# A mixer, attention and mixture-of-experts layer on one core: the gate as one activation, and the whole down product ahead of the remaining transposes

## What is computed

```python
p = softmax(q @ k.T * HD ** -0.5)            # 4 heads, 256 memory tokens
o = p @ v
# for each block of up to 128 slots of one expert
gu = xb @ w_gu + b_gu
g, u = gu[:, :D_FF], gu[:, D_FF:]
g = jnp.minimum(g, SWIGLU_LIMIT)
u = jnp.clip(u, -SWIGLU_LIMIT, SWIGLU_LIMIT)
h = (u + 1.0) * (g * jax.nn.sigmoid(SWIGLU_ALPHA * g))     # SWIGLU_ALPHA = 1.702
return h @ w_down + b_down
```

## Time and profile before

| | |
|---|---|
| median of 3 runs | 2306.88 us (2304.44 to 2308.20) |
| profiled execution | 2305.12 us |
| its span, first to last instruction | 2303.4 us |
| mean granted TensorE clock | 0.975 |
| TensorE, VectorE, ScalarE busy | 2187.8, 1662.6, 1261.9 us |
| instructions | 33358 |

### The profile page before, as it was taken

How to read it: one execution, slowest core, us unless ns; L and a number is a source line. 1 busy time by engine, 2 the same in 40 slices (tenths; PEclk the granted TensorE clock), 3 DMA queues, 4 the chain that set the end, 5 groups by cost and what they waited for, 6 DMA issues and landing times.

```text
span 2303.4 us, 33358 instructions
## 1 busy us (share of the span) xinstructions
PE 2187.8 (95%) x9450; PEld 1665.3 (72%) x9451; DVE 1662.6 (72%) x1641; ACT 1261.9 (55%) x1192; POOL 425.3 (18%) x357
## 2 busy tenths in 40 slices
PE   7999999998998699999999999999999999999986
PEld 4555678886454588877787878788778787887873
DVE  5655842406134899887789977998889779997883
ACT  3146251413213477666567756776677567775663
POOL 0791000000000112122112112221222112221110
PEclk9999999998998799999999999999999999999997
DMA  5103331111123499989799979999899799997984
GB/s 170 37 1 112 110 146 37 37 37 37 57 101 139 170 385 381 324 312 324 244 318 380 369 277 331 350 369 335 311 315 374 275 305 373 380 379 276 311 304 161
DMA packets 233715, 555.95 MB, mean 241 GB/s; under 512 B 19972, under 2 KB 20200, under 8 KB 232200
## 3 DMA queue, kind: packets, MB, share of 16 engines
q1 hardware_dynamic: 218448, 512.41, 61.0%
q0 software_dynamic: 13264, 42.63, 7.4%
q10 hardware_dynamic: 1960, 0.35, 0.1%
HBM read 518.38 MB, written 33.69 MB: 240 GB/s over the span
## 4 chain that ended last, share of the span: by engine, by line
PE 83%; DVE 8%; issue 6%; ACT 2%; DVEq 1%; ACTq 1%; DMA 0%
PE PS L959 21%; PE PS L627 19%; PE PS L963 11%; PE PS L980 11%; PE PS L987 6%; PE PS L785 4%; PE PS L825 4%; DVE WL L1887 2%; PE PS L1012 2%; PE PS L951 2%; PE PS L917 1%; PE PS L645 1%; PE PS L1040 1%; DVE WA L1428 1%; DVE XEL L1883 0%
## 5 line engine op out<-in xcount | busy, mean ns | idle before, releaser
L1887 DVE TENSOR_TENSOR WL<-WA,WH 128x2048 fp32r<-128x2048 f32 x288 | 654.7, 2286 | 66.1 <-ACT WH L1327 62.8
L1887 DVE TENSOR_TENSOR WL<-H,WH 128x2048 fp32r<-128x2048 f32 x144 | 329.3, 2288 | 55.3 <-ACT WH L1306 48.0
L959 PE MATMUL PS<-WH,XEH 128*128 128x512 f32 x1344 | 361.7, 391 | 0.0
L1327 ACT CAST WH<-WA 128x2048 fp32r<-128x2048 f32 x140 | 267.2, 1909 | 164.2 <-PE PS L987 162.2
L963 PE MATMUL PS<-WL,XEH 128*128 128x512 f32 x1344 | 351.9, 389 | 0.0
L959 PE MATMUL PS<-WH,XEL 128*128 128x512 f32 x1152 | 309.4, 390 | 0.0
L959 PEld LDWEIGHTS PS<-WH,XEH 128*128 128x128 f32 x1344 | 253.5, 189 | 51.6
L963 PEld LDWEIGHTS PS<-WL,XEH 128*128 128x128 f32 x1344 | 252.7, 188 | 52.7
L959 PEld LDWEIGHTS PS<-WH,XEL 128*128 128x128 f32 x1152 | 217.2, 189 | 46.1
L980 PE MATMUL PS<-WH,HTH 128*128 128x512 f32 x672 | 191.0, 407 | 6.3 <-DVE WL L1887 6.3
L1311 ACT CAST WH<-WA 128x2048 fp32r<-128x2048 f32 x72 | 137.2, 1910 | 76.2 <-PE PS L963 75.8
(11 more groups left out here) (323 smaller groups left out, 2931.5 us busy)
## 6 DMA issues: line engine op xcount, KB each, us to landing
WA<-in_exp_w_gu SPq DMA_DIRECT2D x216, 1024.0 KB, 7.4
H<-in_exp_w_gu SPq DMA_DIRECT2D x72, 1024.0 KB
WA<-in_exp_w_down SPq DMA_DIRECT2D x72, 1024.0 KB, 7.3
H<-in_exp_w_down SPq DMA_DIRECT2D x72, 1024.0 KB, 8.3
WB<-in_xa_wkv SPq DMA_DIRECT2D x4, 2048.0 KB, 7.9
WB<-in_w_in SPq DMA_DIRECT2D x3, 2048.0 KB, 9.3
y_acc<-H SPq DMA_DIRECT2D x9, 512.0 KB, 2.6
H<-in_x SPq DMA_DIRECT2D x4, 1024.0 KB, 6.0
```

Source lines behind the costliest of these rows:

```text
L959: nc.tensor.matmul(PS[:, 2 * h + t, :], x[:, KT4 * half + k, t * P:(t + 1) * P], WH[:, j % 4, k * HALF:(k + 1) * HALF], start=False, stop= ...
L1327: nc.scalar.copy(WH[:, s, :], raw_gu(s)).then_inc(gu_high, 1)
L1887: v.tensor_tensor(WL[:, s, :], src, WH[:, s, :].bitcast(F32), sub).then_inc(done, 1)
```

## The change

It has five parts.

1. The gate: sigmoid on ScalarE into `SIG` and product on VectorE become one activation in place, `Gelu_apprx_sigmoid` (x times sigmoid of 1.702 x), with one semaphore (`gate_done`) for two; its table is loaded ahead of the loop in place of the sigmoid's. `gate_times` goes. The upper rows of the up product now have a buffer of their own, `UPH`.
2. TensorE's round: both pairs of down slices directly behind one another; token transposes of half 1 and both groups of hidden transposes behind them.
3. VectorE's round: low tokens of half 0 ahead of `down_low(3)`; `down_low(2)` keeps its place ahead of `hidden` of half 1.
4. Attention: the copies of the transposed weights (`keep`) move from VectorE to ScalarE, behind the exponentials.
5. `GF3` is made on ScalarE ahead of the loop and not on VectorE after it.

```diff
@@ -394,8 +394,8 @@
-        g_min, sig_done, gs_done, u_clip, h_done = (
-            sem("g_min"), sem("sig_done"), sem("gs_done"), sem("u_clip"), sem("h_done"))
+        g_min, gate_done, u_clip, h_done = (
+            sem("g_min"), sem("gate_done"), sem("u_clip"), sem("h_done"))
@@ -1017,9 +1017,9 @@
                 by_tiles(pe, n_n, next_tokens(0))
                 by_tiles(pe, n_p, down(0))
+                by_tiles(pe, n_p, down(2))
                 by_tiles(pe, n_n, next_tokens(1))
                 by_tiles(pe, n_i, hidden_transposes(0))
-                by_tiles(pe, n_p, down(2))
                 by_tiles(pe, n_i, hidden_transposes(1))
@@ -1239,6 +1239,13 @@
+            def keep(n):
+                l, hp = att[n]
+                u = ("pt", l, hp)
+                wait_filled(act, u)
+                evac(act, nc.scalar.copy(PT[:, 2 * hp:2 * hp + 2, :, l * P:(l + 1) * P],
+                                         bank(u).rearrange("p (h m t) -> p h m t", h=2, m=MT)), u)
@@ -1253,6 +1260,10 @@
+                if n >= LEAD:
+                    keep(n - LEAD)
+            for n in range(len(att) - LEAD, len(att)):
+                keep(n)
@@ -1275,7 +1286,7 @@
-                    nc.scalar.preload_act_table(ACT.Sigmoid)
+                    nc.scalar.preload_act_table(ACT.Gelu_apprx_sigmoid)
@@ -1293,6 +1304,9 @@
+            act.wait_ge(gf_done, 1)
+            nc.scalar.copy(GF3.rearrange("p l (r e) -> p l r e", r=3), GF.unsqueeze(2).to_broadcast([P, L, 3, E])) \
+                .then_inc(gf3_done, 1)
@@ -1333,17 +1347,15 @@
                     act.wait_ge(g_min, 4 * i + 2 * half + 2)
-                    act.wait_ge(gs_done, 2 * i + half + 1)
                     for t in range(tiles):
                         n = HP if t else P
-                        ins = nc.scalar.activation(SIG[0:n, t, :], HS[0:n, t, half * HALF:(half + 1) * HALF], ACT.Sigmoid,
-                                                   scale=ALPHA)
-                    ins.then_inc(sig_done, 1)
+                        g_t = HS[0:n, t, half * HALF:(half + 1) * HALF]
+                        ins = nc.scalar.activation(g_t, g_t, ACT.Gelu_apprx_sigmoid)
+                    ins.then_inc(gate_done, 1)
                 def upper_up(half):
                     act.wait_ge(gu_used, 8 * i + 4 * half + 8)
-                    act.wait_ge(gs_done, 2 * i + half + 2)
-                    nc.scalar.copy(SIG[0:HP, 1, :], PS[HP:P, 3, :]).then_inc(halves_moved, 1)
+                    nc.scalar.copy(UPH[0:HP, :], PS[HP:P, 3, :]).then_inc(halves_moved, 1)
@@ -1725,20 +1737,11 @@
-            for n in range(len(att) + LEAD):
+            for n in range(len(att) + 1):
                 if n < len(att):
                     maxima(n)
-                if 0 < n <= len(att):
+                if n > 0:
                     normalise(n - 1)
-                if n >= LEAD:
-                    keep(n - LEAD)
@@ -1933,26 +1935,18 @@
-                def gate_times(half, tiles):
-                    dve.wait_ge(sig_done, 2 * i + half + 1)
-                    for t in range(tiles):
-                        n = HP if t else P
-                        g_t = HS[0:n, t, half * HALF:(half + 1) * HALF]
-                        ins = v.tensor_tensor(g_t, g_t, SIG[0:n, t, :], mul)
-                    ins.then_inc(gs_done, 1)
-                    dve.wait_ge(gs_done, 2 * i + half + 2)
+                    dve.wait_ge(gate_done, 2 * i + half + 1)
@@ -1963,7 +1957,6 @@
                     gate_up_low(5)
-                    gate_times(0, tiles)
                     gate_up_low(6)
@@ -1992,14 +1985,12 @@
                     down_low(1)
-                by_tiles(dve, n_i, lambda tiles: gate_times(1, tiles))
-                with dve.If_cmp(n_p, 0, "IS_GT"):
                     down_low(2)
                 by_tiles(dve, n_i, lambda tiles: hidden(1, tiles))
                 counts.fetch(i)
+                by_tiles(dve, n_n, next_tokens(0), lambda: dve.sem_inc(xel_done, 1))
                 with dve.If_cmp(n_p, 0, "IS_GT"):
                     down_low(3)
-                by_tiles(dve, n_n, next_tokens(0), lambda: dve.sem_inc(xel_done, 1))
@@ -2022,7 +2013,6 @@
             dve.sem_inc(loop_left, 1)
-            d(v.tensor_copy(GF3.rearrange("p l (r e) -> p l r e", r=3), GF.unsqueeze(2).to_broadcast([P, L, 3, E])), gf3_done)
```

More of the change, by code:

```diff
@@ L263, in build @@
         HS = wa(12288, 2, D)
-        SIG = wa(14336, 2, HALF)
+        UPH = wa(14336, HALF)
         xn_rows = nc.dram_tensor("xn_rows", (T, D), F32).ap()
@@ L1890, in _ @@
             dve.sem_inc(htl_done, 2)
-            dve.sem_inc(gs_done, 1)
             for j in range(4):
@@ L1949, in hidden @@
                         dve.wait_ge(halves_moved, 4 * i + 2 * half + 2)
-                        v.tensor_tensor(PS[0:HP, 3, :], PS[0:HP, 3, :], SIG[0:HP, 1, :], add).then_inc(u_clip, 1)
+                        v.tensor_tensor(PS[0:HP, 3, :], PS[0:HP, 3, :], UPH[0:HP, :], add).then_inc(u_clip, 1)
                         v.tensor_scalar(PS[:, 2, :], PS[:, 2, :], LIMIT, -LIMIT, ALU.min, ALU.max)
```

## The result

The median went from 2306.88 us to 2351.56 us (2348.89 to 2351.63 in three runs): a ratio of 1.019, 95% interval 1.017 to 1.021. The profiled execution took 2351.56 us, 46.5 more than the 2305.1 of before. The forecast, 2329, has the right sign and about half the size, and the time lies 1.6 us beyond the end of the range.

A forecast was written before the change was run, and what follows sets the result against it. TensorE, busy 95% of the span, was taken as the bound. Bubbles 54.8, less 43.7 removed, plus 17 lateness, plus 1.6 clock, less 5.7 attention gave +24.0 us on 2305.1: 2329 us, range 2308 to 2350.

The forecast's parts named there:

- (a): End of an ordinary round: hand-overs behind the down product add 1.35 us, less 0.12 for one restart fewer.
- (b): Queues of ScalarE and VectorE behind the bubble: first up product 0.34 us late, ordinary round 1.57 longer, 34.5 us in all.
- (c): Other rounds: one-tile before two-tile +11.6 us, two-tile +10.7, outer loop's turn partly in the bubble -2.
- (d): What goes: 12 waits for low tokens (28 us), half clock behind them, L951 waits and restarts; together 43.7 us.
- (e): Lateness left around two-tile rounds: 2.34 us in 6 rounds plus 3, sum 17 us; one clock fall, 1.6.
- R3: Rival, slower still: the bubble lets TensorE's clock fall in 14 rounds, +22 us, 2350 us; chance 0.17.
- (f): Gate as one activation, taken at 0.63 us: direct gain 0 in ordinary rounds.
- R4: Rival: gate activation and copies share no table, 144 loads, 185 us on ScalarE, about 2400 us; chance 0.03.
- (g): Attention copies on ScalarE: value product starts at 560.7 us, -5.7 us, between 0 and -9.
- (h): `GF3` on ScalarE ahead of the loop: cost 0, at most 1 us; no gain at the tail.

The follow-up runs named there:

- e1: The changed kernel with TensorE's round in the order of before, second down half behind the first hidden transposes: 2289.2 us, ratio 0.992.
- e10: The changed kernel with two more pairs of branches on TensorE's sequencer behind each round's last transposes: 2387.0 us, ratio 1.035.
- e3: e1 with VectorE's low tokens of half 0 back behind `down_low(3)`: 2296.4 us, ratio 0.995.
- e4: The kernel before with only the copies of transposed attention weights moved to ScalarE: 2298.6 us, ratio 0.997.
- e6: The changed kernel with eight unread register moves per round, which the program that ran did not hold: 2351.2 us, ratio 1.020.
- e9: e3 with the first hidden transposes moved between slices 2 and 3 of the down product: 2286.8 us, ratio 0.991.
- e12: e9 with VectorE's low tokens of half 1 and `low_hidden(0)` ahead of `gate_up_low(9)`: 2265.3 us, ratio 0.983.

## Why the prediction was half right

It was right in what happens and wrong in how much. Round by round, from the two traces (the forecast is the round of before, less the waits that were to go, plus the step's sum):

| round | times | before | forecast | after |
|---|---|---|---|---|
| ordinary | 7 | 35.5 | 37.1 | 37.4 to 37.5 |
| ordinary, the outer loop turns | 3 | 36.0 | 37.3 | 38.0 |
| next item has two tiles | 5 | 36.3 to 36.5 | 38.2 | 38.8 to 39.3 |
| two tiles | 6 | 54.2 to 55.9 | 54.0 | 53.6 to 53.7 |
| long down product | 6 | 42.6 | 44.7 | 45.0 to 45.6 |
| the one after that | 6 | 39.1 to 41.0 | 39.5 | 39.1 to 39.9 (one of 41.0) |

Left out are the second round, which starts at half clock in both, and of after the four rounds in which the clock fell (1.6 more each).

- **(a), the bubble.** Each of the four hand-overs fell within 0.02 us of its forecast. The step that failed is "the next round's first gate matmul, which waits for that, starts at 2.58": it took the gate for ready as soon as its data are. It started at 3.29, because the sequencer begins the end of the round only when the low tokens come: 0.94 us of it (3.29 less 2.00 and 0.35) are no longer hidden. The term, 1.35 us a round, should have been 2.06. In the earlier trace rows the gate follows the last transposes at once, and I read that as "costs nothing" instead of "is hidden".
- **(b).** The 0.34 at the first up product did not come: the gate started 0.71 later, and with it the product that wanted the value. The queues behind were right (`gate_up_low(10)` at T+3.55 as worked out). Together (a) and (b) made an ordinary round 1.9 longer, not 1.57: the first was 0.71 too small, and the second, which did not come, made up for half of that.
- **(c).** The two-tile rounds came out 0.4 shorter than forecast, the rounds before them 0.6 longer, 1.1 where the outer loop turns. "Now partly lies in the bubble: -2" was the wrong way round: the turn of the outer loop stands behind the wait and cost 0.55 us where it had cost 0.45.
- **(d).** Right that they go: none of the 12 waits is left, and every wait of L1012 in the loop is one of the new bubbles. But they were not 28 us. Of the 28.5 in the earlier trace rows, 5.0 are two waits of the first round; the other 11 are 23.4, and the twelfth is a line that the earlier trace rows leaves out:

```profile
PE PS L1012 <- DVE XEH L1883: 1.6, 1, 1.6
```

  That makes 25.0, and 3.0 us of the forecast's gain were a misread list. And their clock came back, see the next point.
- **(e).** In the round after the long down product TensorE stood idle 0.7 us for the clipped gate on the average of six, and 0.3 for the hidden values; the forecast had 1.70 and 0.64. A TensorE that comes 0.7 later at every gate is waited for by the queues that were to be late: by the lengths of these rounds, against rounds of their kind, 14 us were 11. The clock term failed: one fall of 1.6 us was counted; four stretches at half clock came in these 34 rounds and a fifth in the last live round, as many as the kernel before had. One of them, by the columns of the earlier trace rows:

```profile
1738.60:1741.90 3.30, 3.30 (x9) 2.55 (x8) 3.30 (x2) 2.99 (x3) 0.00 (x0) 0.50 1.02 375
```

  Three more than forecast in the 34 rounds are 4.9 us, the one behind them 1.6. The argument was that the longest idle piece is 1.1 us "with transposes around it"; in fact a bubble holds two pieces, and in many rounds longer ones. Of the 34 rounds' bubbles 13 hold 0.96 and 0.63 to 0.68 us, 1.6 together, and behind none of them did the clock fall; 15 hold 1.8 to 2.6 together, where a piece is longer by the next item's second tile, by a late low part or by the outer loop, and behind five of those it fell. (That is no limit: in e1 it fell behind two bubbles of 1.6.) R3 gave the right time, 2350, by luck, for a reason that is not the main one: it had the clock fall in 14 rounds, and it fell in 5. Its mechanism is real, and it grows with the bubble: e10, whose bubbles are 0.82 longer, shows 0.50 in 16 stretches of these 34 rounds, two of them twice as long; at 1.6 and some 2.7 us of delay that is about 28 us. The mean clock of 850 to 2230 us, in e10 and in after:

```profile
850.00:2230.00 1380.00, 1301.22 (x5840) 1065.46 (x5839) 1094.32 (x786) 883.63 (x669) 203.27 (x206) 0.98 0.90 313
```

```profile
850.00:2230.00 1380.00, 1316.60 (x5987) 1075.97 (x5986) 1116.55 (x799) 903.89 (x685) 213.83 (x210) 1.00 0.92 321
```

  The Trainium skill ("TensorE: Matmul & The Clock Gate", HAM oscillation) tells of a wait in each turn of a loop that throttles the clock in each turn; the trace of after has it in 5 turns of 35, each behind one of the longer bubbles.
- **(f).** Right: no stall at the gate, one activation of 0.63 us on ScalarE, no table load in the loop (R4 falls). By e3, which has the gate, attention and `GF3` but the old orders, against e4, the gate is worth 2 us of the median, 8.5 of the loop in the two traces; part of that is fewer falls of the clock (2 for 5).
- **(g).** Right in sum, with luck in the size: the value product started at 564.34 in a trace that runs 2.1 us later from the start of the scores on, where 566.38 was the earlier trace rows:

```profile
564.34 4.05 PE L627 MATMUL PS<-XT,WA 128*128 128x512 f32 x5 [1.71 <-ACT XT L1246]
```

  That is 4.2 us less for the stretch, where the steps gave 5.7, and 1.5 less at half clock, which the steps had left out: -5.7 as forecast, and -8 in e4's median. In the profiled run of after 1.7 were given back at 625 us by a longer stretch at half clock.
- **(h).** Right, no cost.

The sum over the loop's 34 rounds was forecast at +29.7 and was +46.3. Of the 16.6 between them, the clock is 4.9, the misread waits of (d) 3.0, and the sequencer, less what it spared in (b) and (e), about 9. Outside the loop -5.7 was forecast, and 0.2 came: -5.7 of attention were made up by the 1.7 given back, 2.1 that the trace of after is late from its first 50 us on, and 1.7 for a fall of the clock in the last live round. The 2.1 are not the change's: e6, the same program, is not late there and starts its value product at 562.35. The trace of after has 3.4 us at half clock from 28 us on, which e6's has not.

## What to carry to other kernels

- A bubble at the end of a loop's turn costs its data hand-overs and the sequencer's work behind it. In a round without idle time that work shows as zero, but the trace lists the sequencer's instructions there, too: in the kernel before they took 1.2 us from L455 to L942.
- Give an instruction that waits on other engines a place where its semaphore comes before its turn, and earlier by as much as the sequencer has to do behind it (here 1.3 us, 1.8 where the outer loop turns, less the 0.35 of the transposes). Here one slice of the down product (2.8 us) behind the first hidden transposes and one weight less ahead of the second low tokens removed all such waits.
- When an engine is always late, taking work off it moves the lateness to its next debt (e1, e9); the order of its queue decides who pays (e12).

## What the runs showed of the hardware that was not expected

- TensorE's sequencer did nothing while the transposes at which it stood waited for the low tokens (35 waits in after, no instruction of its own in them), and went on 0.06 us after these were made. From there it needed 1.3 us to the first matmul of the next round, 0.41 us for each further question about the tiles, 0.55 for the turn of the outer loop. In the ordinary rounds of the kernel before, where the low tokens came 1.1 us ahead of the transposes' turn, the first showed as 0.
- The granted clock fell to 0.50 behind 5 of the 15 bubbles of after that hold 1.8 to 2.6 us of idle time in two pieces, and behind none of the 13 that hold 1.6. In e10, whose bubbles are longer, it fell behind 4 of the 15 of 2.4 us and behind all 13 of 2.6 to 3.4.
- Eight register moves a round whose result is never read cost nothing (2351.2 against 2351.6 us), since they are not in the program that ran: 32993 instructions with and without them.
